# Moving one of four depthwise-convolution tiles from VectorE to GpSimd

## What is computed

```python
CONV_CH = D_MODEL // 2          # 512 channels
CONV_WIDTH = 31
MLA_HEADS = 8

def conformer_conv(conv_in, conv_w, conv_b, ln_g, ln_b, w_conv_out):
    a, gt = jnp.split(conv_in, 2, axis=-1)
    z = a * jax.nn.sigmoid(gt)
    rhs = conv_w.astype(z.dtype).reshape(CONV_WIDTH, 1, CONV_CH)
    z = lax.conv_general_dilated(
        z, rhs, window_strides=(1,), padding=[(CONV_WIDTH - 1, 0)],
        dimension_numbers=("NWC", "WIO", "NWC"), feature_group_count=CONV_CH)
    z = z + conv_b
    z = layer_norm(z, ln_g, ln_b)
    z = jax.nn.silu(z)
    return z @ w_conv_out

def first_block(...):
...
        conv_out = conformer_conv(conv_in, ...)
        mla_out = mla_attention(c_q, c_kv, k_rope_raw, ...)
        gates = jax.nn.sigmoid(gate_logits).reshape(B, S, N_BRANCH, D_MODEL)
        merged = gates[:, :, 0] * conv_out + gates[:, :, 1] * mla_out
        h = h + merged @ w_out[l]
```

## Time and profile before

| | us |
|---|---|
| three runs: lowest, median, highest | 1510.06, 1513.34, 1514.72 |
| the profiled execution, its own time | 1509.91 |
| its span, first to last instruction | 1508.2 |
| TensorE busy | 1462.3 (97%) |
| VectorE busy | 789.5 (52%) |
| ScalarE busy | 577.0 (38%) |
| GpSimd busy | 102.6 (7%) |

### The profile page before, as it was taken

How to read it: one execution, slowest core, us unless ns; L and a number is a source line. 1 busy time by engine, 2 the same in 40 slices (tenths; PEclk the granted TensorE clock), 3 DMA queues, 4 the chain that set the end, 5 groups by cost and what they waited for, 6 DMA issues and landing times.

```text
span 1508.2 us, 20254 instructions
## 1 busy us (share of the span) xinstructions
PE 1462.3 (97%) x6907; PEld 1177.3 (78%) x6907; DVE 789.5 (52%) x1232; ACT 577.0 (38%) x949; POOL 102.6 (7%) x83
## 2 busy tenths in 40 slices
PE   6999999899899999999999999999999999999997
PEld 5788877677867888888888777787787887878885
DVE  4538888775456544254445574344444344345552
ACT  5434444434545442124333353333333333333232
POOL 0000000101303000000033220000000000000001
PEclk9999999999999999999999999999999999999999
DMA  4322213223412333323323232221222312213231
GB/s 145 86 70 69 73 45 92 70 81 115 140 42 84 86 97 96 110 75 95 110 84 93 60 105 61 79 87 56 87 72 67 91 42 87 87 56 98 86 97 70
DMA packets 242783, 126.16 MB, mean 84 GB/s; under 512 B 17026, under 2 KB 241363, under 8 KB 242738
## 3 DMA queue, kind: packets, MB, share of 16 engines
q1 hardware_dynamic: 242162, 123.47, 28.3%
q10 hardware_dynamic: 576, 2.10, 0.4%
HBM read 123.45 MB, written 2.10 MB: 83 GB/s over the span
## 4 chain that ended last, share of the span: by engine, by line
PE 70%; issue 17%; DVE 4%; POOL 4%; ACT 2%; DMA 2%; SPq 0%; POOLq 0%; DVEq 0%; ACTq 0%
PE lin L556 20%; PE lin L560 19%; PE lin L559 19%; PE sc L633 3%; PE ob L647 3%; PE tr L641 1%; DVE wl L1394 1%; POOL kt L531 1%; ACT wh L1026 1%; POOL logit L538 1%; POOL qt L531 1%; PE tr L598 1%; PE sc L693 1%; DMA raw<-in_w_xkv_dram 1%; PE sc L598 1%
## 5 line engine op out<-in xcount | busy, mean ns | idle before, releaser
L1394 DVE TENSOR_TENSOR wl<-raw,wh 128x1024 fp32r<-128x1024 f32 x238 | 292.1, 1237 | 189.7 <-ACT wh L1026 185.2
L556 PE MATMUL lin<-uh,wh 128*128 128x512 f32 x752 | 304.2, 404 | 4.6 <-DVE pt L1867 2.0
L560 PE MATMUL lin<-uh,wl 128*128 128x512 f32 x752 | 294.1, 391 | 0.0
L559 PE MATMUL lin<-ul,wh 128*128 128x512 f32 x752 | 293.7, 390 | 0.0
L1026 ACT ACTIVATE wh<-raw 128x1024 fp32r<-128x1024 f32 x238 | 239.0, 1012 | 130.8 <-DMA raw<-in_w_mlp_dram 42.4
L556 PE MATMUL lin<-vh,wh 128*128 128x512 f32 x576 | 238.8, 415 | 1.7 <-DVE pt L1867 0.9
L559 PE MATMUL lin<-vl,wh 128*128 128x512 f32 x576 | 227.4, 395 | 0.0
L560 PE MATMUL lin<-vh,wl 128*128 128x512 f32 x576 | 227.3, 395 | 0.0
L556 PEld LDWEIGHTS lin<-uh,wh 128*128 128x128 f32 x752 | 141.7, 188 | 39.0 <-issue 4.6
L559 PEld LDWEIGHTS lin<-ul,wh 128*128 128x128 f32 x752 | 141.8, 189 | 29.8 <-issue 2.6
L560 PEld LDWEIGHTS lin<-uh,wl 128*128 128x128 f32 x752 | 141.5, 188 | 30.3
(11 more groups left out here) (356 smaller groups left out, 1721.1 us busy)
## 6 DMA issues: line engine op xcount, KB each, us to landing
raw<-in_w_in_dram SPq DMA_DIRECT2D x101, 512.0 KB, 3.6
raw<-in_w_mlp_dram SPq DMA_DIRECT2D x64, 512.0 KB, 4.0
raw<-in_w_out_dram SPq DMA_DIRECT2D x16, 512.0 KB, 3.5
raw<-in_w_xkv_dram SPq DMA_DIRECT2D x8, 512.0 KB, 3.5
raw<-in_w_proj_b_dram SPq DMA_DIRECT2D x8, 512.0 KB, 3.5
raw<-in_w_proj_a_dram SPq DMA_DIRECT2D x8, 512.0 KB, 3.5
xtok<-in_x_dram ACTq DMA_DIRECT2D x4, 512.0 KB, 5.1
raw<-in_w_mla_out_dram SPq DMA_DIRECT2D x4, 512.0 KB, 3.8
```

Of the source, the lines that this page charges most:

```text
L556: ins = pe.matmul(o, wh[:, slot, at], xh_, start=start, stop=False)
L559: pe.matmul(o, wh[:, slot, at], xl_, start=False, stop=False)
L560: return pe.matmul(o, wl[:, slot, at], xh_, start=False, stop=stop)
L1394: dve.tensor_tensor(wl[:, c.slot(4), 0:size], raw[:, c.slot(2), 0:size], wh[:, c.slot(4), 0:size].bitcast(F32), ALU.subtract).then_inc(lo_ ...
```

## The change

Tile 3 of the convolution goes to GpSimd. It waits for all four tiles of `z`, and then does for tap 0 one instruction (multiply and add the bias, into `acc` 3), and for each of the 30 other taps two: a product into `ta` or `tb` in turn, and an addition to `acc` 3, with a wait on its own semaphores between them. After that it makes `conv_total` from `acc` 3 and `acc` 0, and adds 1 and 2.

VectorE keeps tiles 0 to 2, 96 steps. The loop over pairs of heads is gone; all eight heads are written out, with 12 steps each, 4 in every `run`. Tiles now cross the borders between heads. Before the subtraction of the mean VectorE waits for GpSimd's tile as well.

```diff
--- before.py
+++ after.py
@@ -289,6 +289,7 @@
         u_made, u_high, u_low = sem("u_made"), sem("u_high"), sem("u_low")
         kr_ready, kr_placed = sem("kr_ready"), sem("kr_placed")
         z_made, tap_done = sem("z_made"), sem("tap_done")
+        pool_product, pool_tap_done = sem("pool_product"), sem("pool_tap_done")
         vtr_ready, vtok_placed = sem("vtr_ready"), sem("vtok_placed")
         bias_made = sem("bias_made")
         scores_ready, logits_made, probs_made = sem("scores_ready"), sem("logits_made"), sem("probs_made")
@@ -501,11 +502,26 @@
 
             add_squares("q")
             add_squares("kv")
-            pool.wait_ge(tap_done, 2 * (TAPS + 1))
-            pool.tensor_tensor(conv_total[:], acc[:, 0, :], acc[:, 1, :], ALU.add).then_inc(conv_added, 1)
-            for t in range(2, CT):
+            pool.wait_ge(z_made, CT)
+            pool.wait_ge(vec_copied, 2)
+            last = acc[:, CT - 1, :]
+            for w in range(TAPS):
+                zt, tap_ = z[:, CT - 1, w:w + S], taps[:, TAPS * (CT - 1) + w:TAPS * (CT - 1) + w + 1]
+                if w == 0:
+                    pool.tensor_scalar(last, zt, tap_, col("conv_b", CT - 1), ALU.mult, ALU.add)\
+                        .then_inc(pool_tap_done, 1)
+                else:
+                    part = (ta, tb)[w % 2]
+                    pool.tensor_scalar(part[:], zt, tap_, None, ALU.mult).then_inc(pool_product, 1)
+                    pool.wait_ge(pool_product, w)
+                    pool.wait_ge(pool_tap_done, w)
+                    pool.tensor_tensor(last, last, part[:], ALU.add).then_inc(pool_tap_done, 1)
+            pool.wait_ge(pool_tap_done, TAPS)
+            pool.wait_ge(tap_done, TAPS + 1)
+            pool.tensor_tensor(conv_total[:], last, acc[:, 0, :], ALU.add).then_inc(conv_added, 1)
+            for t in range(1, CT - 1):
                 pool.wait_ge(tap_done, (t + 1) * (TAPS + 1))
-                pool.wait_ge(conv_added, t - 1)
+                pool.wait_ge(conv_added, t)
                 pool.tensor_tensor(conv_total[:], conv_total[:], acc[:, t, :], ALU.add).then_inc(conv_added, 1)
             add_squares("conv")
             add_squares("mem")
@@ -1577,37 +1593,35 @@
                 outputs(n, otok[:, :, at:at + VD] if n.i is None else otok[:, :, bass.ds(at, VD)])
                 lower(c + 6)
 
-            def two_heads(c, j, t, n):
-                def tap(w):
-
-
-                    zt, at = z[:, t, w % TAPS:w % TAPS + S], (acc[:, t, :], te[:])[w % 2]
-                    k = (TAPS + 1) * t + w
-                    tap_ = taps[:, bass.ds(TAPS * t + w % TAPS, 1)]
-                    if w:
-                        dve.wait_ge(tap_done, k - (1 < w < TAPS))
-                    if w == 0:
-                        ins = dve.tensor_scalar(at, zt, tap_, cols[:, bass.ds(COL["conv_b"] + t, 1)], ALU.mult, ALU.add)
-                    elif w == 1:
-                        ins = dve.tensor_scalar(at, zt, tap_, None, ALU.mult)
-                    elif w < TAPS:
-                        ins = dve.scalar_tensor_tensor(at, zt, tap_, at, ALU.mult, ALU.add)
-                    else:
-                        ins = dve.tensor_tensor(acc[:, t, :], acc[:, t, :], te[:], ALU.add)
-                    ins.then_inc(tap_done, 1)
-
-                for p, cuts in ((0, (0, 6, 11, 16)), (1, (16, 22, 27, TAPS + 1))):
-                    head(c + 4 * p, j + 4 * p, n + p, lambda k: [tap(w) for w in range(cuts[k], cuts[k + 1])])
+            def tap(t, w):
+
+                zt, at = z[:, t, w % TAPS:w % TAPS + S], (acc[:, t, :], te[:])[w % 2]
+                k = (TAPS + 1) * t + w
+                tap_ = taps[:, TAPS * t + w % TAPS:TAPS * t + w % TAPS + 1]
+                wait(dve, tap_done, k - (1 < w < TAPS) if w else 0)
+                if w == 0:
+                    ins = dve.tensor_scalar(at, zt, tap_, col("conv_b", t), ALU.mult, ALU.add)
+                elif w == 1:
+                    ins = dve.tensor_scalar(at, zt, tap_, None, ALU.mult)
+                elif w < TAPS:
+                    ins = dve.scalar_tensor_tensor(at, zt, tap_, at, ALU.mult, ALU.add)
+                else:
+                    ins = dve.tensor_tensor(acc[:, t, :], acc[:, t, :], te[:], ALU.add)
+                ins.then_inc(tap_done, 1)
 
             lower(phase("heads")[0] + 2)
-            with dve.Fori(0, CT - 1) as i:
-                two_heads(*phase("heads", 8, 8, i), i, Idx(0, 2, i))
             c, j = phase("heads")
-            two_heads(c + 8 * (CT - 1), j + 8 * (CT - 1), CT - 1, Idx(2 * (CT - 1)))
+            steps = [(t, w) for t in range(CT - 1) for w in range(TAPS + 1)]
+            cuts = (0, 4, 8, 12)
+            for n in range(HEADS):
+                mine = steps[12 * n:12 * n + 12]
+                head(c + 4 * n, j + 4 * n, Idx(n),
+                     lambda k: [tap(t, w) for t, w in mine[cuts[k]:cuts[k + 1]]])
 
 
             dve.wait_ge(mean_ready, 1)
-            dve.wait_ge(tap_done, CT * (TAPS + 1))
+            dve.wait_ge(tap_done, (CT - 1) * (TAPS + 1))
+            dve.wait_ge(pool_tap_done, TAPS)
             for t in range(CT):
                 dve.scalar_tensor_tensor(acc[:, t, :], sc[0][:], -1.0 / CONV, acc[:, t, :], ALU.mult, ALU.add)\
                     .then_inc(centred, 1)
```

## The result

| | before | after |
|---|---|---|
| median of 5 runs, us | 1513.58 | 1522.99 |
| lowest and highest | 1510.06, 1514.94 | 1522.03, 1525.00 |
| profiled execution, its own time | 1509.91 | 1525.00 |
| first `qt` to the product for the mean | 166.67 | 178.21 |

The ratio is 1.0066, with a 95% interval of 1.005 to 1.0082: 9.4 us slower. Of the 15.1 us between their spans 11.5 lie in the heads phase; the other 3.6 lie ahead of it and behind it, where both kernels do the same.

A forecast was written before the change was run, and what follows sets the result against it. TensorE was taken to bound the kernel. Heads growing from 20.54 to 27.5 us, 2.9 x 7.0 = 20.4, less 1.9 gain, gave +18.5: 1509.9 to 1528.4, or 1532 with the median's 3.4 above; range 1522 to 1553.

The forecast's parts named there:

- What bounds the kernel: Heads phase: TensorE is busy for all of a 20.54 us head; VectorE has some 3 us of room.
- the collision: In each head, 16 VectorE instructions alternate with GpSimd's, 0.70 us more a step, 0.77 a large `wl`: 11.2 us.
- The rival in which VectorE keeps its turn: Heads: GpSimd works only in VectorE's gaps, so no change; only the 1.9 us gain remains, 1511.4 us; chance 0.11.
- GpSimd doesn't keep it either: Rival, heads: product and addition both pass before VectorE's turn, +32, 1545 us; chance 0.22 together with dear products.
- The chain of GpSimd: Tile 3 on GpSimd: 61 instructions, about 109 us, products 0.48, additions 1.15; with first sum, 2.9 heads, to about 190 us.
- The upper bound: Heads, with products as dear as additions: a head of 33.1 us, +38 us in all.
- The idle time of VectorE: In each head, of VectorE's 3.02 us wait for ScalarE's `wh`, some 1.8 us stay.
- The end: Last head: TensorE's wait for `pt` shrinks by 0.66 us, the last sum comes 1.32 earlier: gain 1.3 us.
- the waits for `qt`: Heads phase: TensorE's waits for VectorE's `qt` go, a gain of 0.6 us.
- The clock: Rival, first three heads: TensorE stands still 7 us a head, then runs at 1.2 GHz: +39 on top, 1571 us; chance 0.05.
- the signs of being wrong: Profile after: 0.74 us steps beside busy GpSimd, GpSimd beyond 240 us, clock below 0.95 in first heads, or 20.5 us heads throughout.
- the +9 "with half of the collisions missed": Heads: bound in which the two engines don't always ask at once, so half the collisions are missed: about +9 us.

The follow-up runs named there:

- additions only: The change with GpSimd's 30 additions kept and its 30 products left out, the shifted z itself being added: 1526.45 us, ratio 1.0085.
- writes only: The change with GpSimd's chain replaced by 180 iota instructions that write ta and tb and read nothing from SBUF: 1510.52 us, ratio 0.9989.
- The kernel with the faster product: The change with GpSimd's 30 products made as multiply and add 0.0 instead of multiply alone: 1529.32 us, ratio 1.0105.
- the products alone: The change with GpSimd's 30 products kept and its 30 additions left out: 1511.47 us, ratio 0.9992.
- the kernel without the chain: The change with GpSimd's chain cut to its first instruction, taps 1 to 30 of tile 3 left out: 1510.74 us, ratio 0.9988.
- the kernel with `pt` earlier: The change with VectorE's 12 steps dealt 4, 1, 7 and not 4, 4, 4 in the first five heads: 1524.90 us, ratio 1.0096.

## Why the prediction was right, and where it was off

**What bounds the kernel, and the collision: right.** A step of VectorE and a GpSimd addition exclude each other (additions only), a GpSimd instruction that only writes keeps nobody out (writes only), the two engines take turns, and TensorE can't make up what it loses. The rival in which VectorE keeps its turn is out: its steps took 1.77 and 1.17 us from the first head. GpSimd doesn't keep it either; no step waited for an addition and a product together, which would have made it 0.54 + 1.63 = 2.17 us long; the longest took 1.81.

**The chain of GpSimd: the step that failed.** "A product with one tensor input is not in the trace [...] I take 0.48". As the time for which VectorE is kept out this was right. But it was also taken for how long the product lasts, and that is 1.56 us. The estimate of 0.44 us, which the prediction worked out from the Trainium skill ("GPSIMD Engine Reference", section "Elementwise — side-by-side cycle accounting"), is as far off. A tap of GpSimd takes 3.46 us where VectorE has work, and not 1.02 + 1.69 = 2.71, and VectorE gets three steps into it, not two. So a head lost 2.0 to 3.4 us by VectorE's pace (heads of 22.6 to 24.0), and up to 3.6 with the clock, where 7.0 were forecast, and it lasted for four heads and a part of the fifth, where 2.9 were forecast: 9.8 to 13.0 us over the first four heads, in place of 20.4. The kernel with the faster product is the one that the forecast described, and it measures heads of 26.8 to 27.3 us, three of them, and +16.5 us, against 27.5, 2.9 and +18.5. Part of that agreement is luck: 1.1 to 1.6 us of each head are a wait for TensorE at a lowered clock, which the forecast didn't have, and VectorE alone would make them 25.6 to 26.2. The upper bound treated a long product as one that shuts VectorE out as long; the products alone show that it does not.

**The idle time of VectorE: right.** 1.8 us were reckoned to stay of the 3.02, and 1.96 did.

**The end: right.** 1.3 us: the waits shrank by 0.66 and 0.67 us. The 0.6 us for the waits for `qt` came to 0.9 in the kernel without the chain.

**The clock: wrong in its chance, right that it matters little.** A granted clock below 0.95 in the first heads stood among the signs of being wrong, and it came: 0.93. It had been set aside because it was 1.00 in the first 10 us with TensorE idle. That row stands ahead of the first product; within the phase the clock fell to 0.50, the level of 1.2 GHz, behind stalls of 1.27 to 1.76 us. The Trainium skill ("TensorE: Matmul & The Clock Gate", section "HAM oscillation — how this bites in real kernels") says that stalls of TensorE drop its clock to half. The trace of the change agrees, in four heads of four; that of the change run again does so in two of four. The price in the rival supposed three whole heads at the low level; it was some 3 us in a head, mostly under VectorE's own delay.

**The sum.** 1532 was forecast and 1523.0 measured, half of the loss and 1 us above the low end of the range. That it lies inside is partly luck: run again, the change took 1520.48. Of the bounds, the +9 "with half of the collisions missed" comes nearest in number, and in part for a like reason, since a third of the steps meets nothing. But no working stands behind it: in the prediction's own terms half of the collisions would make a head of 14.5 + 5.6 + 1.8 = 21.9 us, 1.4 longer than 20.54, which makes a few us in all and not 9.

## What to carry to other kernels

Before work is moved from VectorE to GpSimd, count VectorE's instructions with two tensors in SBUF in that stage, and read in the trace how long each engine stands still behind the other; it is the time for which the other is held off that counts, not how long GpSimd's instruction lasts. Spread such a chain so thinly that the loss in each period fits in VectorE's idle time: with the same 61 instructions the kernel was 9.4 us slower than before over four heads and 0.6 over seven. And a faster instruction on the side engine can make the kernel slower, since it asks for its turn more often.

## What the runs showed of the hardware that had not been expected

- A GpSimd `tensor_scalar` of 128x512 with a multiply alone takes 1.56 us, with multiply and add 0.70 to 0.77 us. A step of VectorE that meets either takes 1.17 to 1.18 us, 0.44 more than its 0.74, so both keep VectorE out for about 0.5 us.
- The Trainium skill ("SBUF — State Buffer", section "SBUF: two separate sides") has the loser blocked for the whole instruction. For GpSimd's additions that holds (steps of 1.75 us), for its lone products it does not: VectorE ran a whole step of 0.74 us inside one of 1.67.
- TensorE's granted clock fell to 0.50 behind stalls of 1.27 to 1.76 us, but not behind each: in one trace of the change in four heads of four, in another in two. It stayed at 1.00 behind a stall of 3.10 us in the kernel with `pt` earlier. So the length of the stall alone doesn't decide it.
